# Second layer's values one step sooner, seven conv steps earlier, ScalarE's weight parts behind the transposes' copy, spatial products' halves by turns

## The chip, the cores and the metric

The kernel runs on one core of a Trainium2 chip. The metric is the device time of one execution in microseconds (us), the median of several runs. TensorE (PE) multiplies, ScalarE (ACT) and VectorE (DVE) do the element-wise work, GpSimd (POOL) helps a little, and SyncE (SP) issues most of the DMAs. Each engine runs its own instructions strictly in program order and waits on semaphores for the others.

## The reference

Two blocks follow each other. The first is one hybrid layer (dilated attention and a gated recurrence). The second has two layers on 512 tokens and 256 context tokens. The change touches the token mixers of the second block, which do this in each layer:

```
zx = split(hx @ w_in, 10)                    # ten parts of 256 columns
glu = a_val * sigmoid(a_gate)
y_a = silu(layer_norm(depthwise_conv(glu, conv_a_w) + b))        # 31 taps
p1 = softmax(q1 @ k1 * scale); p2 = softmax(q2 @ k2 * scale)
y_b = rms_norm(((p1 - lam * p2) @ v), subln_g) * (1 - lam_init)  # 4 heads
s   = einsum('gpq,bcqgd->bcpgd', w_s, layer_norm(gelu(v)))       # 4 groups of 64
y_c = gelu(u) * (s + b_s)
y_d = bg * depthwise_conv(cg * xin, conv_w)
x   = x + gate * (concat(y_a, y_b, y_c, y_d) @ w_out)
```

Layer 0 of the block also runs the mixers on the 256 context tokens; layer 1 only takes keys and values from them.

## The kernel before

**Weights.** Every large weight matrix comes in chunks of 1 MB (128 partitions x 2048). SP loads chunk n into a ring of three. `split(n)` exists twice: on ScalarE (L2107) it copies the chunk to a high part `whi` in reduced precision, and on VectorE (L2317) it subtracts that from the chunk and gets the low part `wlo`. So VectorE's `split(n)` waits for ScalarE's `split(n)` (semaphore `w_hi`), and PE waits for both before chunk n. Each product takes three matmuls (high x high, low x high, high x low), all recorded at L1957.

**Attention among the projections.** Chunks 5 to 9 of the input projection (j = 5 to 9) are cut into 16 steps each, 80 in all; a step is three matmuls of 512 columns (in layer 0 also three of 256 for the context). `fill(g)` puts attention work before step g. The attention of a layer is cut in units, one for 128 queries of one head: 16 in layer 1 (four a head), 20 in layer 0 (a fifth one a head for the context, with narrower tiles). A unit v starts at step `start(v)`, three steps after the one before it. On PE it has three pieces:

- `scores` at start - 3 (L624 to L627): four matmuls, q1 k1 and q2 k2. It waits for both exponentials of the unit before (`q_e`).
- `turn` at start + 2 (L643): six transposes of the combined probabilities. It waits for `combine` of its unit (`q_w`) and for the output of the unit before to be stored (`q_on`).
- `values` at start + 4 (L652, context units L658): twelve short matmuls. It waits for the copy of the transposes (`q_pt`).

Between them VectorE takes the maxima (L1351), ScalarE two exponentials with sums (L964, `exp(v, 0)` and `exp(v, 1)`), VectorE combines (L1365, L1366, L1371), ScalarE copies the transposes (L991, `out`) and stores the result scaled (L981, `scaled`). A round of ScalarE's loop `run` is `exp(v+1, 0)`, `scaled(v-1)`, `exp(v+1, 1)`, `out(v)`. A round of VectorE's is `combine(v)`, `maxima(v+1)`, then either a waiting weight split or three steps of the 31-tap convolution (L1247), whose 62 steps also fill earlier gaps. The units run in two batches: the first `cut` units (15 in layer 0, 12 in layer 1), and after the norms and spatial products the rest.

**Evictions.** `upto(g)` in ScalarE's and VectorE's loops empties the accumulators of the projection when its steps are due; after the second half of a chunk ScalarE calls `split(n + 2)` at once, while VectorE only notes it and does it after the next `maxima` (`weights_due`).

**Spatial products.** `s_mixed` (L703) multiplies a 64-column weight tile with 128 columns for each token block j and group g; groups 0 and 2 write partitions 0 to 63, groups 1 and 3 write 64 to 127. All j of one group come first, then the next group.

Of the kernel before, what the change touches and what calls it, by code (L numbers as in the profile page):

```python
# [157 lines left out]
class Plan:  # L158
# [21 lines left out]
        return self.start(v) + 2  # L180

    def values(self, v):
        return self.start(v) + 4


PLAN = [Plan(_l) for _l in range(L2)]
# [84 lines left out]
def build(nc, wst, mst, cbt, vec, xrs, xin, cin, gst, cst, msk, rop, row, sgw, sgb, out):  # L271
    with ExitStack() as ctx:
# [305 lines left out]
        def layer(pe, l, gemm, norm_sums, norm_spread, wait_high, wait_low, weights, step, half_gemm,  # L578
# [5 lines left out]
            nj = 6 if l == 0 else 4  # L584
# [110 lines left out]
            def s_mixed():  # L695
                pe.wait_ge(s_nat, l + 1)
                pe.wait_ge(m_t, 2 * l + 2)
                for c in (1, 0):
                    for g in (2 * c, 2 * c + 1):
                        half = 64 * (g % 2)  # L700
                        for j in range(nj):
                            o = (turned, score)[c][half:half + 64, j * P:(j + 1) * P]
                            last = pe.matmul(o, snat[:, j, 64 * g:64 * g + 64], wsT[:, g, :], start=True, stop=True)  # L703
                    last.then_inc(s_mix, 1)

            def fill(g):


                for v in range(p.units):
                    if g == p.scores(v):  # L710
                        scores(v)
                    if g == p.values(v):
                        values(v)
                    if g == p.turned(v):
                        turn(v)
                if g == p.mean:
                    means()
                if g == p.sums:
                    variances()
                if g == p.spread:  # L720
                    spread()
                if g == p.mix:
                    s_mixed()
# [147 lines left out]
        def layer_act(act, l, split, norm_square, norm_root, norm_high, mod_shift, half_square, half_root,  # L871
# [47 lines left out]
            def evict(j, c):  # L919


                n = base + j
                if j == 5:
                    act.wait_ge(qk_kept[0], 32 * (l + 1))
                    act.wait_ge(stacked[0], 16 * stacks_in(l, 0))
                    act.wait_ge(acc_ready[c], n + 1)
                    if two and c:
                        act.activation(svn[:, 4:6, :], ctx_acc, ACT.Copy).then_inc(ctx_out, 1)
                    act.activation(svn[:, 2 * c:2 * c + 2, :].rearrange("p b f -> p (b f)"), acc[:, c, 0:T], ACT.Copy
                                   ).then_inc(acc_free[c], 1)  # L930
                elif j < 8:
                    dst = (ug, cx)[j - 6]
                    o = 1 if j == 7 else 0
                    if j == 6:
                        act.wait_ge(qk_kept[1], 32 * (l + 1))
                    if j == 7:
                        act.wait_ge(cx_zero, l + 1)
                    act.wait_ge(acc_ready[c], n + 1)
                    if two and c:
                        oc = T + (3 if j == 7 else 0)  # L940
                        act.activation(dst[:, :, oc:oc + TC], ctx_acc, ACT.Copy).then_inc(ctx_out, 1)
                    act.activation(dst[:, c, o:o + T], acc[:, c, 0:T], ACT.Copy).then_inc(acc_free[c], 1)
                if c and j < 9:
                    split(n + 2)

            done = [0]

            def upto(g):


                while done[0] + 8 < g and done[0] < 80:
                    done[0] += 8
                    evict(5 + (done[0] - 8) // 16, (done[0] - 8) // 8 % 2)
# [49 lines left out]
            def run(v0, v1):  # L1003


                for part in range(2):
                    exp(v0, part)
                for v in range(v0, v1):
                    if v + 1 < v1:
                        exp(v + 1, 0)  # L1010
                    if v > v0:
                        scaled(v - 1)
                    if v + 1 < v1:
                        exp(v + 1, 1)
                    if p.turned(v) < 80:
                        out(v)

            run(0, p.cut)
            scaled(p.cut - 1)
# [4 lines left out]
            ins.then_inc(gelus, 1)  # L1024
            act.activation(ug[:, :, 0:wx], ug[:, :, 0:wx], ACT.Gelu_apprx_tanh).then_inc(gelus, 1)
            upto(p.mean)
            act.wait_ge(m_cen, l + 1)
            act.activation(sqm[:, :, 0:wx], yca[:, :, 0:wx], ACT.Square).then_inc(m_sq, 1)
            act.activation(unread[:, l:l + 1], epsc, ACT.Sqrt)
# [8 lines left out]
            act.wait_ge(sv_squared, l + 1)  # L1038
            act.activation(sv_sd[:, 0:nj], sv_sq[:, 0:nj], ACT.Sqrt, bias=epsc, scale=1.0 / GW).then_inc(sv_root, 1)
            upto(p.sums)  # L1040
            root_o(0)
            upto(p.spread)

            def affine(c, src, func, g, b):
                act.activation(src[:, c, 0:wx], src[:, c, 0:wx], func, bias=vcol(b, c, 1), scale=vcol(g, c, 1)
# [2 lines left out]
            for c in range(2):  # L1048
                act.wait_ge(m_t, 2 * l + c + 1)
                affine(c, yca, ACT.Silu, f"lag{l}", f"lab{l}")  # L1050
            upto(p.mix)
            run(p.cut, p.units)
            upto(89)

            def y_high(i):

# [135 lines left out]
        def layer_dve(dve, link, l, split, norm_inverse, norm_scale, modulate, modulation, coefficients,  # L1192
# [59 lines left out]
            for j in range(5):  # L1252
# [17 lines left out]
                if j > 2:  # L1270
                    rotate(j - 3)
                    if j == 4:
                        split(n + 1)
                    low(j - 3)
                    conv((7, 9)[j - 3] if two else 11)
                if j < 3:
                    split(n + 2)

# [1452 lines left out]
```

## Time and profile before

| | us |
|---|---|
| runs | 2112.39, 2116.89, 2120.92 |
| median | 2116.89 |
| profiled execution | 2115.37 |
| its span | 2113.5 |
| PE busy in the span | 2040.2 |

The span runs from the first to the last instruction; 1.87 us of the profiled execution lie around it. Busy times of matmuls contain their pipelined tails, so a busy PE may still have room. The attention of layer 0 lies at 712 to 871 us of the span, that of layer 1 at 1573 to 1694 us.

### The profile page before, as it was taken

What the parts mean: (1) busy time and instruction counts of PE and PEld (TensorE: products, weight loads), DVE (VectorE), ACT (ScalarE), POOL (GpSimd) and SP (SyncE); (2) the same over time, 40 slices, a digit from 0 to 9 for tenths busy, and PEclk for the clock granted to TensorE, in tenths of its full rate; (3) what the DMA queues carried; (4) which work ended last, traced back from release to release, by engine and by line L of the source; (5) the groups of instructions that cost most, each with busy time, mean ns of one, the idle gap of its engine ahead of it and who ended that gap; (6) DMA issues with size and microseconds to landing.
All of it is one profiled execution on the core that took longest, in us unless ns stands there. A gap on an engine that the chain in (4) does not pass through costs nothing.

```text
span 2113.5 us, 26503 instructions
## 1 busy us (share of the span) xinstructions
PE 2040.2 (97%) x11156; PEld 1739.0 (82%) x11156; DVE 1270.3 (60%) x1696; ACT 795.1 (38%) x1117; POOL 72.4 (3%) x81
## 2 busy tenths in 40 slices
PE   6999999999999999999999999999998999999998
PEld 5989888778788888887888888888787787888887
DVE  7466866867657885727546455464689645344343
ACT  4333334584343455534113122132536534132231
POOL 0000000000120000020000000001100010000001
PEclk9999999999999999999999999999999999999999
DMA  8643523525322531222333232232353122232221
GB/s 290 224 159 120 213 86 129 186 90 188 131 100 74 162 92 70 70 82 98 111 111 120 90 120 100 100 122 105 112 167 90 70 90 89 91 100 100 100 95 65
DMA packets 54054, 249.18 MB, mean 118 GB/s; under 512 B 6224, under 2 KB 12512, under 8 KB 35504
## 3 DMA queue, kind: packets, MB, share of 16 engines
q1 hardware_dynamic: 52048, 242.41, 33.4%
q10 hardware_dynamic: 1296, 2.63, 0.3%
q0 software_dynamic: 592, 2.46, 0.3%
q8 instruction: 88, 1.44, 0.3%
q14 instruction: 30, 0.25, 0.0%
HBM read 232.53 MB, written 12.06 MB: 116 GB/s over the span
## 4 chain that ended last, share of the span: by engine, by line
PE 85%; DVE 9%; ACT 3%; issue 2%; DMA 1%; POOL 0%; ACTq 0%; DVEq 0%; POOLq 0%
PE banks L1957 70%; DVE small L1351 2%; PE banks L1981 1%; PE banks L1982 1%; PE banks L1983 1%; PE banks L652 1%; PE banks L531 1%; ACT whi_f L2107 1%; PE banks L643 1%; DVE wlo_f L2317 1%; DVE ntx L2351 1%; PE banks L607 1%; PE banks L606 1%; PE banks L608 1%; PE banks L2013 1%
## 5 line engine op out<-in xcount | busy, mean ns | idle before, releaser
L1957 PE MATMUL banks<-hxh,whi_f 128*128 128x512 f32 (+1 forms) x1464 | 585.4, 400 | 24.3 <-ACT hxh L2136 7.5
L1957 PE MATMUL banks<-hxh,wlo_f 128*128 128x512 f32 (+1 forms) x1464 | 569.7, 389 | 0.0
L1957 PE MATMUL banks<-hxl,whi_f 128*128 128x512 f32 (+1 forms) x1464 | 555.2, 388 | 0.2 <-DVE hxl L2386 0.2
L2317 DVE TENSOR_TENSOR wlo_f<-raw_f,whi_f 128x2048 fp32r<-128x2048 f32 x133 | 304.9, 2293 | 181.4 <-ACT whi_f L2107 181.2
L2107 ACT ACTIVATE whi_f<-raw_f 128x2048 fp32r<-128x2048 f32 x133 | 253.7, 1907 | 308.3 <-PE banks L1957 290.1
L1957 PEld LDWEIGHTS banks<-hxh,whi_f 128*128 128x128 f32 x1464 | 276.1, 189 | 86.6 <-issue 27.5
L1957 PEld LDWEIGHTS banks<-hxh,wlo_f 128*128 128x128 f32 x1464 | 275.8, 188 | 57.9
L1957 PEld LDWEIGHTS banks<-hxl,whi_f 128*128 128x128 f32 x1464 | 274.9, 188 | 58.0 <-issue 1.9
L1957 PE MATMUL banks<-fxh,whi_f 128*128 128x512 f32 (+1 forms) x528 | 205.6, 389 | 2.1 <-DVE cT L1495 1.1
L1957 PE MATMUL banks<-fxh,wlo_f 128*128 128x512 f32 (+1 forms) x528 | 204.2, 387 | 0.0
L1957 PE MATMUL banks<-fxl,whi_f 128*128 128x512 f32 (+1 forms) x528 | 203.5, 385 | 0.0
L1495 DVE SCALAR_TENSOR_TENSOR xT<-banks,small,xT 128x512 f32<-128x512 f32 x76 | 56.5, 750 | 239.4 <-PE banks L1957 239.4
L1569 DVE TENSOR_TENSOR fsq<-relu 128x768 f32<-128x768 f32 (+1 forms) x64 | 52.7, 824 | 165.5 <-ACT relu L1149 165.5
L1149 ACT ACTIVATE relu<-banks 128x768 f32<-128x768 f32 (+1 forms) x64 | 45.1, 704 | 281.6 <-PE banks L1957 281.6
L1957 PE MATMUL banks<-hch,whi_f 128*128 128x256 f32 x464 | 132.7, 286 | 0.0
L1957 PE MATMUL banks<-hch,wlo_f 128*128 128x256 f32 x464 | 130.5, 281 | 0.0
L1957 PE MATMUL banks<-hcl,whi_f 128*128 128x256 f32 x464 | 130.0, 280 | 0.0
L1957 PEld LDWEIGHTS banks<-fxh,whi_f 128*128 128x128 f32 x528 | 99.2, 188 | 28.0 <-issue 4.8
L2337 DVE SCALAR_TENSOR_TENSOR mvr<-mvr,c2b 128x1024 f32<-128x1024 f32 x96 | 117.1, 1220 | 0.0
L1957 PEld LDWEIGHTS banks<-fxl,whi_f 128*128 128x128 f32 x528 | 99.2, 188 | 20.8
L1957 PEld LDWEIGHTS banks<-fxh,wlo_f 128*128 128x128 f32 x528 | 99.2, 188 | 20.4
L1247 DVE SCALAR_TENSOR_TENSOR aconv<-gpad,vecs,aconv 128x798 f32<-128x798 f32 (+1 forms) x120 | 99.6, 893 | 0.0
(340 smaller groups left out, 3129.3 us busy)
## 6 DMA issues: line engine op xcount, KB each, us to landing
raw_f<-in_wst SPq DMA_DIRECT2D x133, 1024.0 KB, 4.9
mvr<-in_mst SPq DMA_DIRECT2D x120, 512.0 KB, 5.8
stack<-qk_parts SPq DMA_DIRECT2D x36, 192.0 KB, 6.6
x_kept<-xT SPq DMA_DIRECT2D x2, 2048.0 KB, 8.6
raw_f<-in_wst SPq DMA_DIRECT2D x8, 384.0 KB, 5.9
xT<-x_kept SPq DMA_DIRECT2D x2, 1536.0 KB, 8.7
qk_parts<-qk_h SPq DMA_DIRECT2D x3, 768.0 KB, 3.8
qk_parts<-qk_l SPq DMA_DIRECT2D x3, 768.0 KB, 3.6
```

What stands on the lines that cost most here:

```text
L531: last = pe.matmul(at_ov, vb[h // 2][:, i, j, d], pt[:, u % 2, b * P:(b + 1) * P], start=(b == 0), stop=(b == 5))
L606: pe.matmul(place(b), hi[:, k, o:o + P], wh[:, k, :], start=(k == 0), stop=False)
L607: pe.matmul(place(b), lo[:, k, o:o + P], wh[:, k, :], start=False, stop=False)
L1149: act.activation(relu[:, c, 0:wx], acc[:, c, 0:wx], ACT.Relu).then_inc(acc_free[c], 1)
L1247: ins = dve.scalar_tensor_tensor(aconv[:, c, 0:wc], gpad[:, c, tap:tap + wc], w, aconv[:, c, 0:wc], ALU.mult, ALU.add)
L1351: dve.tensor_reduce(dnm[:, z:z + 2], score.rearrange("p (i k) -> p i k", i=2), AX_X, ALU.max, negate=True).then_inc(q_m, 1)
L1495: ins = dve.scalar_tensor_tensor(x_, acc[:, c, o:o + w], small[:, bass.ds(2 * t + g0, 1)], x_, ALU.mult, ALU.add)
L1569: dve.tensor_tensor(fsq[:, c, 0:wx], relu[:, c, 0:wx], relu[:, c, 0:wx], ALU.mult).then_inc(f_sq, 1)
L1957: last = pe.matmul(o, (wh, wl)[w][:, k, c, :], r[part][:, k, :], start=(k == order[0] and parts is not LOW and (w, part) == (0, 0)), stop= ...
L2107: act.activation(whi[n % 2 if n > N_FIRST else n][:], raw[w_place(n)][:], ACT.Copy).then_inc(w_hi, 1)
L2317: dve.tensor_tensor(wlo[r][:], raw[r][:], whi[n % 2 if n > N_FIRST else n][:].bitcast(F32), ALU.subtract).then_inc(w_lo, 1)
L2337: dve.scalar_tensor_tensor(w, w, 1.0, c2[:, 1], ALU.mult, ALU.mult, accum_out=mvc[:, col + 1:col + 2]).then_inc(mv_used, 1)
```

## The change

There are five edits.

1. In layer 1 `values(v)` moves from start + 4 to start + 3. At that step `scores(v+2)` also stands; `fill` now goes over all scores first, so that scores come ahead of the values.
2. In layer 1 ScalarE does `scaled(v-1)` ahead of `exp(v+1, 0)`; in layer 0 it stays between the exponentials.
3. ScalarE's `split(n + 2)` in chunks 5 to 8 is no longer done at the eviction: it is noted and done at `weights_due`, which stands at the end of a round of `run` behind `out(v)`, and at some places between the batches. VectorE's code for its own splits is as before.
4. In layer 1 the convolution does 14 and 15 steps instead of 11 and 11 during chunks 3 and 4, so seven fewer are left for the attention's rounds.
5. `s_mixed` loops over j outside and the two groups inside, so that the two halves of the partitions come by turns.

```diff
     def values(self, v):
-        return self.start(v) + 4
+        return self.start(v) + (4 if self.per == 5 else 3)
...
                 for c in (1, 0):
-                    for g in (2 * c, 2 * c + 1):
-                        half = 64 * (g % 2)
-                        for j in range(nj):
+                    for j in range(nj):
+                        for g in (2 * c, 2 * c + 1):
+                            half = 64 * (g % 2)
...
                 for v in range(p.units):
                     if g == p.scores(v):
                         scores(v)
+                for v in range(p.units):
                     if g == p.values(v):
                         values(v)
...
                 if c and j < 9:
-                    split(n + 2)
+                    weights_due()
+                    due[0] = n + 2
+
+            due = [None]
+
+            def weights_due():
+                if due[0] is not None:
+                    split(due[0])
+                due[0] = None
...
                 for v in range(v0, v1):
+                    if v > v0 and not two:
+                        scaled(v - 1)
                     if v + 1 < v1:
                         exp(v + 1, 0)
-                    if v > v0:
+                    if v > v0 and two:
                         scaled(v - 1)
                     if v + 1 < v1:
                         exp(v + 1, 1)
                     if p.turned(v) < 80:
                         out(v)
+                    weights_due()
...
-                    conv((7, 9)[j - 3] if two else 11)
+                    conv((7, 9)[j - 3] if two else (14, 15)[j - 3])
```

`weights_due()` is also called on ScalarE after `upto(p.mean)`, `upto(p.sums)`, `upto(p.spread)`, `upto(p.mix)` and `upto(89)`.

PE in layer 1, one round of the first batch. `whi_f,hxh` and the two beside it are the projection's step, `stack` the scores, `consts,prob` the transposes, `vnat,ptd` the values. Before:

```order
L643 MATMUL banks<-consts,prob 128x128 [waits diff_on,diff_pt,diff_w]
L643 MATMUL banks<-consts,prob 128x128 x5
L1957 MATMUL banks<-hxh,whi_f 128x512
L1957 MATMUL banks<-hxl,whi_f 128x512
L1957 MATMUL banks<-hxh,wlo_f 128x512
L624 MATMUL banks<-stack_127 128x512 [waits diff_e]
L625 MATMUL banks<-stack_127 128x256
L626 MATMUL banks<-stack_127 128x256
L627 MATMUL banks<-stack_127 128x512
L1957 MATMUL banks<-hxh,whi_f 128x512
L1957 MATMUL banks<-hxl,whi_f 128x512
L1957 MATMUL banks<-hxh,wlo_f 128x512
```

The values came behind that last step. Now the place from the scores on reads:

```order
L625 MATMUL banks<-stack_127 128x256
L626 MATMUL banks<-stack_127 128x256
L627 MATMUL banks<-stack_127 128x512
L652 MATMUL banks<-vnat,ptd 128x64 [waits diff_pt]
L652 MATMUL banks<-vnat,ptd 128x64 x5
L1976 MATMUL banks<-hxh,whi_f 128x512
L1976 MATMUL banks<-hxl,whi_f 128x512
L1976 MATMUL banks<-hxh,wlo_f 128x512
```

Two steps of the projection now stand between the values and the next transposes, where one stood before.

ScalarE in layer 1 at the end of chunk 6 (`ug` is its eviction), where the high part of chunk 8 is due; the two `prob` rows are the exponentials of unit 10, the `ptd` row behind them is the copy of unit 9's transposes, and `onat` is `scaled(8)`. Before:

```order
L942 ACTIVATE ug<-banks 128x512 [waits acc_ready1,qk_kept1]
L2107 ACTIVATE whi_f<-raw_f 128x2048 [waits acc_ready1,w_loaded1]
L964 ACTIVATE prob,small<-banks,small 128x768 [waits diff_t,diff_m]
L981 ACTIVATE onat<-banks,small 128x64 [waits diff_o]
L964 ACTIVATE prob,small<-banks,small 128x768
L991 ACTIVATE ptd<-banks 128x768 [waits diff_o,diff_t]
```

Now:

```order
L943 ACTIVATE ug<-banks 128x512 [waits acc_ready1,qk_kept1]
L992 ACTIVATE onat<-banks,small 128x64 [waits diff_o]
L975 ACTIVATE prob,small<-banks,small 128x768 [waits diff_t,diff_m]
L975 ACTIVATE prob,small<-banks,small 128x768
L1002 ACTIVATE ptd<-banks 128x768 [waits diff_o,diff_t]
L2126 ACTIVATE whi_f<-raw_f 128x2048 [waits acc_ready1,w_loaded1]
```

The high part went from ahead of unit 10's exponentials to behind them and behind the copy. Layer 0 has the same move at its chunk 6, with the same units.

VectorE at that place, the same before and now (line numbers of the changed kernel): the maxima of unit 10, the low part of chunk 8, the combining of unit 10.

```order
L1370 TENSOR_REDUCE small<-banks 128x2 [waits diff_s]
L2336 TENSOR_TENSOR wlo_f<-raw_f,whi_f 128x2048 [waits w_hi]
L1384 RECIPROCAL small<-small 128x2 [waits diff_on,diff_e]
L1385 SCALAR_TENSOR_TENSOR small<-small 128x1 [waits dve_step]
L1390 SCALAR_TENSOR_TENSOR prob<-prob,small 128x768 [waits dve_step]
```

Nothing moved here: the low part, which waits for the high part, stands ahead of unit 10's combining.

## Rows read from the trace of the kernel before

**Rows 1.** The page, part 1: engine, busy us, share of the span, instructions.

```profile
PE 2040.2 (97%) x11156; PEld 1739.0 (82%) x11156; DVE 1270.3 (60%) x1696; ACT 795.1 (38%) x1117; POOL 72.4 (3%) x81
```

**Rows 2.** PE's waits at 1560 to 1640: us in total, times, longest.

```profile
PE banks L643 <- ACT onat L981: 4.6, 9, 0.9
PE banks L624 <- ACT prob L964: 3.1, 2, 1.6
```

**Rows 3.** Timeline, layer 1, one round: start, us, engine, line, instruction [idle before <- releaser].

```profile
1594.39 0.17 DVE L1365 RECIPROCAL small<-small 128x2 f32<-128x2 f32 x1 [0.16 <-ACT prob L964]
...
1595.02 0.40 PE L624 MATMUL banks<-stack 128*128 128x512 f32 x1
...
1595.93 1.76 DVE L1351 TENSOR_REDUCE small<-banks 128x2 f32<-128x1536 f32 x1
...
1597.72 0.90 ACT L964 ACTIVATE prob<-banks,small 128x768 f32<-128x768 f32 x1 [2.40 <-DVE small L1351]
...
1598.61 0.30 ACT L981 ACTIVATE onat<-banks,small 128x64 f32<-128x64 f32 x1
...
1599.06 0.85 PE L643 MATMUL banks<-consts,prob 128*128 128x128 f32 x6 [0.42 <-ACT onat L981]
...
1599.83 0.17 DVE L1365 RECIPROCAL small<-small 128x2 f32<-128x2 f32 x1
```

**Rows 4.** Timeline, layer 1: two combinings with no `onat` row between them.

```profile
1578.60 0.15 DVE L1365 RECIPROCAL small<-small 128x2 f32<-128x2 f32 x1
...
1583.66 0.17 DVE L1365 RECIPROCAL small<-small 128x2 f32<-128x2 f32 x1
```

**Rows 5.** Timeline, layer 1, units 10 and 11 of the first batch.

```profile
1629.13 1.91 ACT L2107 ACTIVATE whi_f<-raw_f 128x2048 fp32r<-128x2048 f32 x1
...
1631.07 2.29 DVE L2317 TENSOR_TENSOR wlo_f<-raw_f,whi_f 128x2048 fp32r<-128x2048 f32 x1
...
1639.94 1.45 PE L652 MATMUL banks<-vnat,ptd 128*128 128x64 f32 x12
...
1641.98 0.82 PE L643 MATMUL banks<-consts,prob 128*128 128x128 f32 x6
```

**Rows 6.** Timeline, layer 0, unit 10 of the first batch.

```profile
773.28 1.93 ACT L2107 ACTIVATE whi_f<-raw_f 128x2048 fp32r<-128x2048 f32 x1
...
776.76 2.28 DVE L2317 TENSOR_TENSOR wlo_f<-raw_f,whi_f 128x2048 fp32r<-128x2048 f32 x1
...
778.96 0.60 ACT L991 ACTIVATE ptd<-banks 128x512 f32<-128x512 f32 x1
778.99 0.17 DVE L1365 RECIPROCAL small<-small 128x2 f32<-128x2 f32 x1
...
784.05 0.85 PE L643 MATMUL banks<-consts,prob 128*128 128x128 f32 x6 [0.40 <-ACT onat L981]
```

**Rows 7.** Timeline of VectorE alone, layer 1, chunks 3 to 5.

```profile
1555.72 0.69 DVE L1223 SCALAR_TENSOR_TENSOR tmp<-banks,rope 128x512 f32<-128x512 f32 x1 [2.74 <-issue]
...
1563.58 7.37 DVE L1247 SCALAR_TENSOR_TENSOR aconv<-gpad,vecs,aconv 128x512 f32<-128x512 f32 x11
1574.72 1.76 DVE L1351 TENSOR_REDUCE small<-banks 128x2 f32<-128x1536 f32 x1 [3.77 <-PE banks L627]
```

**Rows 8.** Timeline, layer 1: two runs of PE with 64-column weight tiles.

```profile
1647.85 0.66 PE L676 MATMUL banks<-wsT,consts 128*64 128x128 f32 x8
...
1660.21 2.57 PE L703 MATMUL banks<-wsT,snat 128*64 128x128 f32 x32
```

**Rows 9.** Windows: stretch, its us, busy us of PE, PEld, DVE, ACT, POOL, granted clock, DMA.

```profile
868.40:871.90 3.50, 1.83 (x13) 1.49 (x13) 2.72 (x6) 3.50 (x9) 0.00 (x0) 1.00 0.96 372
871.90:875.30 3.40, 3.40 (x11) 2.92 (x12) 3.40 (x7) 3.35 (x7) 0.00 (x0) 0.50 0.91 352
875.30:878.70 3.40, 3.40 (x21) 2.94 (x20) 3.30 (x8) 3.16 (x5) 0.00 (x0) 1.00 0.02 5
1576.00:1579.40 3.40, 1.79 (x13) 1.50 (x13) 3.33 (x5) 1.88 (x4) 0.00 (x0) 1.00 1.05 259
```

More of the change, by code:

```diff
@@ L1026, in layer_act @@
             upto(p.mean)
+            weights_due()
             act.wait_ge(m_cen, l + 1)
@@ L1040, in layer_act @@
             upto(p.sums)
+            weights_due()
             root_o(0)
             upto(p.spread)
+            weights_due()
             def affine(c, src, func, g, b):
@@ L1051, in layer_act @@
             upto(p.mix)
+            weights_due()
             run(p.cut, p.units)
             upto(89)
+            weights_due()
             def y_high(i):
```

## The prediction

> **What bounds the kernel now.** I read the page first: PE is busy for 2040.2 of 2113.5 us [rows 1]. What it does not idle away cannot be won by moving work of the other engines, so the waits of PE are all there is to gain. Next its waits in layer 1's first batch of attention: nine times 4.6 us before the transposes (`turn`) on the stored output of the unit before, and 3.1 us before the scores of units 1 and 2 on the exponentials [rows 2]. Then the timeline of one round, to see what sets its length. The reader should follow the circle there: VectorE combines from 1594.39, takes the next maxima from 1595.93, ScalarE starts `exp` at 1597.72, stores the output at 1598.61 (0.20 us between its start and the second `exp`), and the next combining starts at 1599.83, 5.44 us after the last [rows 3]. Where no output is stored between the exponentials, a round takes 1583.66 - 1578.60 = 5.06 us [rows 4]. PE has slack: the transposes wait 0.42 us [rows 3]. So a round in layer 1 is bound by the circle VectorE - ScalarE, with PE close behind.
>
> **Edits 1 and 2 in layer 1, the gain.** The output is stored while ScalarE waits 2.40 us for the maxima [rows 3], so the 0.20 us leave the circle. The values end earlier by a step, so that this output is ready in that gap. What is late next is the circle itself at 5.06 us: combining 1.4, maxima 1.8, two exponentials 1.85. PE's own work per round is 5.44 less the wait of 0.42, so 5.0 us at most; it just fits. The round shortens by 0.38 us. Eight rounds lie between unit 2 and unit 10; an eviction between the exponentials (about 0.5 us in two of them) leaves the circle too, and one round carries a weight split on VectorE and gains little. 7 x 0.38 + 2 x 0.5 = 3.7 us; at unit 10 PE and VectorE should be about 3.5 us ahead of before. The bounds: nothing, if PE's switch between kinds of work keeps it at 5.4, and the 4.6 us of waits at most. In the second batch I find 0.3 us for the few rounds and give back as much at its end, since the values now come so soon behind the transposes that they wait about 0.4 us for the copy (0.8 us). That is 0.
>
> **Edit 3, the move that costs.** ScalarE's high parts have four places per layer in question. At three of them the high part moves by a copy or a norm's worth of work and VectorE asks for it only later; I cost them at nothing, since the low parts there stand behind maxima or norms that end later anyway. The fourth is chunk 6's end, unit 10, in both layers. Before, the high part starts at 1629.13 and the low part on VectorE at 1631.07, right after the maxima, in the time in which ScalarE takes the exponentials [rows 5]. Now the high part stands behind both exponentials and the copy, while the low part still stands ahead of the combining of unit 10. VectorE therefore waits on that semaphore, and queued behind it are the combining, the next maxima and all that hangs on them; PE's next transposes wait for the combining.
>
> Layer 0: the copy starts at 778.96 and takes 0.5 us on ScalarE; the high part (1.93) then ends at 781.4, the low part (2.28) at 783.7 where the combining now starts at 778.99 [rows 6]. Then 1.4 combining, 1.8 maxima, 0.9 for the first `exp`, and, since layer 0 keeps the output behind that `exp`, 0.6 until PE may turn: 788.4 against 784.05 [rows 6]. PE had 0.40 us of waiting there, which is in the 784.05. So **+4.4 us**, all on the path, as nothing later in that layer waits long enough to give it back.
>
> Layer 1, with the 3.5 us of head start: unit 10's exponentials 1627.8 to 1629.7, copy to 1630.5, high part to 1632.4, low part to 1634.7, combining to 1636.2 (PE has waited 3 us at the transposes). The maxima of unit 11 and its exponentials end at 1639.7, the copy of unit 10 at 1640.5, and only then come the values of unit 10, which before started at 1639.94 [rows 5] (PE waits another 3 us). From the values to the next transposes lie 1.25 + two steps of 0.7 + 0.1, so they start at 1643.2 instead of 1641.98 [rows 5]. The values of unit 11 wait 0.4 us for their copy. Sum **+1.6 us**: the head start of 3.5 is spent and more. Without the head start it would be +5.1.
>
> **Edit 4.** Three steps at chunk 3 and four at chunk 4. A step is 7.37 / 11 = 0.67 us [rows 7]. VectorE idles 2.74 us ahead of the rotation at 1555.72 and 3.77 us ahead of the first maxima at 1574.72 [rows 7]: 2.0 and 2.7 us fit. Nothing is paid; without that cover it would be 4.7 us. In the rounds the steps ran beside the exponentials, so removing them from units 8 on brings nothing either. **0**.
>
> **Edit 5.** 32 records of `s_mixed` take 2.57 us, of which the last one's own length is 0.27: 2.30 / 31 = 0.074 us each. The 8 records at L676 already have their halves by turns: (0.66 - 0.27) / 7 = 0.056 us each [rows 8]. Layer 0 has 48 records and layer 1 has 32: 80 x 0.018 = 1.5 us. I take **-1.5**, with 0 and -3 as ends (no effect; half of all), as L676 is the nearest row: same tile, same columns. The Trainium skill (TensorEngine Tiling (Array Packing), Key Properties) says that different tiles can load weights and multiply in parallel, up to twice as fast by its table; by that rule the edit would bring some 3 us, and L676 with 0.056 rather than 0.037 speaks for less.
>
> **The clock.** In this trace the granted clock fell to 0.50 at 871.9 to 875.3, after a stretch of 3.5 us in which PE was busy for 1.83 us only; 11 matmuls ran there and 21 in the equal stretch behind it, so it cost half of 3.4, 1.7 us [rows 9]. At 1576.0 PE was busy for 1.79 of 3.4 us and the clock stayed [rows 9], so the fall is not certain. The three new waits (4.7, 3 and 3 us) are emptier than either stretch. The middle one has another wait behind it that hides a slow stretch. I take one fall on the path, **+1.7**, with 0 and 5 as ends. The Trainium skill (TensorE: Matmul & The Clock Gate, Why this matters for your kernels) warns of gaps in PE's work for this reason; the trace agrees at 871.9.
>
> **Sum.** 4.4 + 1.6 + 0 + 0 - 1.5 + 1.7 = +6.2 us. Against the profiled execution, 2115.4 + 6.2 = 2121.6 us (span 2119.7 and 1.87 around it). That execution lies 1.5 below the median of the runs, 2116.9, and the runs spread from 2112.4 to 2120.9, so 1.5 more or less is in the measure of before itself.
>
> **The rivals.** *Forecast:* the low part waits behind the late high part in both layers and eats more than the shorter rounds give. For it speaks the order of the rows on both engines, which nothing at run time changes. 2121.6, own range 2117 to 2126.
>
> *The rounds win.* If PE were not held by VectorE at unit 10 (its transposes of unit 10 being covered by something that I count as serial), the stalls would vanish and the rest stay: -3.5 (edit 1 and 2) - 1.5 = -5.0, 2110.4. Against it: PE's slack per round is 0.4 us and the delay 4.7. A half of it, the stall in layer 0 only, gives 2115.4 + 4.4 - 3.5 - 1.5 = 2114.8.
>
> *The clock falls for longer.* At the three new waits, and once more in layer 1, PE runs at half clock for a stretch of 3.4 us behind each: 4 x 1.7 = 6.8 instead of 1.7, and the head start in layer 1 is only half (+1.8). 4.4 + 3.4 - 1.5 + 6.8 = +13.1, 2128.5. It decides from the fourth stretch on, since two falls give 2123 and three 2125. For it: three waits of a kind that the trace of before does not have. Against it: the waits of 1.6 us before units 1 and 2 left the clock alone.
>
> *The edit does less than it says.* Rounds stay at 5.4 and the halves by turns bring nothing: 4.4 + 5.1 + 1.7 = +11.2, 2126.6.
>
> **How the numbers follow.** Forecast 0.62, the edit does less 0.12, the clock for longer 0.11, the rounds win or half of it 0.15. The likeliest is 2121.6 us. For the range I leave out the full win (below 2112) and the longest clock falls: 2112.5 to 2128. About 0.5% of the time, 10.6 us, is what a measurement can tell from no change: faster needs less than 2106.3, which no case reaches (0.02 for what I overlook); slower needs over 2127.5, the clock's case and the upper tail of the one before it (0.15); the same, 0.83.
>
> **What would show it.** In layer 1 the distance from one combining to the next should read about 5.1 us instead of 5.44 up to unit 9, with the output's row in the gap ahead of the exponentials. At unit 10 of each layer VectorE should idle 4 us or so ahead of the low part, released by ScalarE's high part, and PE 3 to 5 us ahead of the transposes. The seven convolution steps should leave idle time of 0.7 and 1.1 us where they now stand. `s_mixed` should take 1.8 to 2.0 us in layer 1. A clock of 0.50 should stand behind the wait in layer 0. The prediction is wrong if VectorE's low part finds its high part ready, or if the transposes of unit 10 start on time.

## The result, and the profile after

The kernel after takes **2129.6 us** (median of 5 runs, 2126.5 to 2131.4) against 2120.2 us for the kernel before (5 runs): ratio 1.0048, interval 1.0032 to 1.0064. Run once more on another chip it was 2131.0 against 2119.0 (1.0059, 1.0044 to 1.0073). It is slower by 0.5%, and lies above the forecast of 2121.6 and above the whole range (2112.5 to 2128.0). The profiled execution took 2126.5, its span 2124.7 against 2113.5 before.

The whole kernel on one line, page part 1, to set beside [rows 1]:

```profile
PE 2048.7 (96%) x11156; PEld 1748.2 (82%) x11156; DVE 1270.1 (60%) x1696; ACT 795.6 (37%) x1117; POOL 72.5 (3%) x81
```

PE has the same 11156 instructions and is *busy* for 8.5 us longer. Waits would show as idle time; busy time that grows for the same instructions means that some of them ran slower. That is the first sign of where the prediction fell short.

PE's waits of the kernel after at 1560 to 1700 (us in total, times, longest), to set beside [rows 2]:

```profile
PE banks L624 <- ACT prob L975: 6.2, 4, 1.7
PE banks L643 <- DVE prob L1390: 2.5, 1, 2.5
PE banks L652 <- ACT ptd L1002: 2.2, 4, 1.5
```

Between 1560 and 1700 the kernel before waits 6.2 us for `prob` ahead of the scores, as here, and 5.8 us in eleven waits for `onat` ahead of the transposes. Those waits for `onat` are gone, as forecast. A round at units 8 and 9 (timeline: start, us, engine, line, instruction [idle before <- releaser]), to set beside [rows 3]:

```profile
1615.60 0.17 DVE L1384 RECIPROCAL small<-small 128x2 f32<-128x2 f32 x1
...
1617.92 0.32 ACT L992 ACTIVATE onat<-banks,small 128x64 f32<-128x64 f32 x1 [1.65 <-PE banks L652]
...
1618.77 0.90 ACT L975 ACTIVATE prob<-banks,small 128x768 f32<-128x768 f32 x1 [0.54 <-DVE small L1370]
...
1620.68 0.17 DVE L1384 RECIPROCAL small<-small 128x2 f32<-128x2 f32 x1
```

From combining to combining are 5.08 us instead of 5.44, and the output is stored in the gap ahead of the exponentials. Now unit 10, layer 0 first, then layer 1 (timeline), beside [rows 6] and [rows 5]:

```profile
783.39 1.91 ACT L2126 ACTIVATE whi_f<-raw_f 128x2048 fp32r<-128x2048 f32 x1
785.33 2.29 DVE L2336 TENSOR_TENSOR wlo_f<-raw_f,whi_f 128x2048 fp32r<-128x2048 f32 x1 [4.55 <-ACT whi_f L2126]
787.54 0.16 DVE L1384 RECIPROCAL small<-small 128x2 f32<-128x2 f32 x1
...
792.25 1.09 PE L643 MATMUL banks<-consts,prob 128*128 128x128 f32 x4 [4.66 <-ACT onat L992]
...
1636.49 1.91 ACT L2126 ACTIVATE whi_f<-raw_f 128x2048 fp32r<-128x2048 f32 x1
1638.44 2.29 DVE L2336 TENSOR_TENSOR wlo_f<-raw_f,whi_f 128x2048 fp32r<-128x2048 f32 x1 [4.44 <-ACT whi_f L2126]
1640.64 0.16 DVE L1384 RECIPROCAL small<-small 128x2 f32<-128x2 f32 x1
1642.17 1.54 PE L643 MATMUL banks<-consts,prob 128*128 128x128 f32 x6 [2.50 <-DVE prob L1390]
...
1646.44 1.55 PE L652 MATMUL banks<-vnat,ptd 128*128 128x64 f32 x12 [1.46 <-ACT ptd L1002]
```

VectorE idles 4.5 us ahead of the low part in both layers, released by the late high part, and PE waits behind it. And the windows of the kernel after (stretch, its us, busy us of PE, PEld, DVE, ACT, POOL, granted clock, DMA), beside [rows 9]:

```profile
741.00:744.40 3.40, 1.73 (x10) 1.62 (x11) 2.96 (x9) 2.01 (x7) 0.00 (x0) 0.94 0.94 355
744.40:747.80 3.40, 3.40 (x15) 2.97 (x14) 0.00 (x0) 2.61 (x2) 0.00 (x0) 0.56 1.03 225
747.80:751.20 3.40, 3.40 (x25) 3.13 (x24) 3.21 (x2) 1.42 (x4) 0.00 (x0) 1.00 0.72 157
788.40:791.80 3.40, 0.00 (x0) 0.00 (x0) 3.40 (x4) 1.09 (x4) 0.00 (x0) 1.00 0.00 0
791.80:795.20 3.40, 2.95 (x11) 2.76 (x12) 3.06 (x5) 2.00 (x5) 0.00 (x0) 0.50 0.00 0
...
1638.30:1641.70 3.40, 1.36 (x6) 0.75 (x5) 3.19 (x4) 0.31 (x2) 0.00 (x0) 1.00 0.31 66
1641.70:1645.10 3.40, 2.82 (x9) 2.00 (x9) 2.08 (x2) 1.29 (x3) 0.00 (x0) 0.50 0.00 0
1645.10:1648.50 3.40, 2.06 (x15) 1.97 (x16) 1.40 (x3) 1.60 (x4) 0.00 (x0) 1.00 0.00 0
1648.50:1651.90 3.40, 3.40 (x13) 2.85 (x12) 0.00 (x0) 1.09 (x2) 0.00 (x0) 0.51 0.02 5
```

A fall of the clock to 0.50 (1.2 of 2.4 GHz) stands behind the wait in layer 0, and two stand behind the waits in layer 1. In all there are **ten** such falls of 3.4 us in this execution (at 611, 744, 792, 833, 881, 1591, 1642, 1649, 1686 and 1771), against the one at 871.9 in the profiled execution before. The fall at 744 follows a wait of 2.1 us for ScalarE's `svn` that the kernel before has too; so not every fall is the change's. The falls at 611 and 833 follow no wait of PE over 0.3 us at all (see the last section). To split luck from cause I used the mean granted clock that each run lists, and experiments.

Laid side by side by VectorE's instructions, the two profiled executions differ like this (after minus before): +0.7 at 600; +4.0 at 760 (the falls at 611 and 744, 1.6 us each); +8.2 right behind the low part of unit 10 and +9.6 behind the fall at 792; +9.2 at 890; +5.4 at 1440 (see the last section); +9.1 at 1660, behind layer 1's first batch; +8.5 behind `s_mixed`; +9.6 at 1700; +11.2 at 1780, behind the fall at 1771, and at the end.

### The profile page after: what moved, and what is told of

The parts are those of the page before. It is cut to its first block, busy times and chain, and to the rows that moved or that the text cites. A ratio compares the mean times of both kernels' runs of the same rounds, so it can differ in the third digit from the quotient of the medians.

```text
span 2124.7 us, 26503 instructions
## 1 busy us (share of the span) xinstructions
PE 2048.7 (96%) x11156; PEld 1748.2 (82%) x11156; DVE 1270.1 (60%) x1696; ACT 795.6 (37%) x1117; POOL 72.5 (3%) x81
## 4 chain that ended last, share of the span: by engine, by line
PE 84%; DVE 9%; ACT 3%; issue 2%; DMA 1%; POOL 0%; ACTq 0%; DVEq 0%; POOLq 0%
PE banks L1976 69%; DVE small L1370 2%; PE banks L2000 1%; PE banks L2001 1%; PE banks L2002 1%; PE banks L652 1%; PE banks L531 1%; ACT whi_f L2126 1%; DVE prob L1390 1%; DVE wlo_f L2336 1%; DMA mvr<-in_mst 1%; DVE aconv L1266 1%; PE banks L606 1%; PE banks L607 1%; PE banks L608 1%
```

## The experiments

Each kernel ran beside the kernel before on one chip; kernels with the same value under "before" shared it. The ratio is not that of the two medians but lies near that of the means; where a kernel's runs are spread wide (e5, e7), the two readings differ by up to 2 us. "Clock" is the mean granted clock over a kernel's timed runs; for the kernel before it was 0.9950 to 0.9954 in the four sets. Over 277 runs of all kernels, a run's distance from its kernel's mean time goes with its distance from its kernel's mean clock at 1.8 us (plus or minus 0.1) for each 0.001 (correlation -0.74), and one fall of 3.4 us is 0.0008 of the clock: some 1.5 us.

| kernel | median us | before | ratio (interval) | clock |
|---|---|---|---|---|
| after, first set | 2129.6 | 2120.2 | 1.0048 (1.0032 to 1.0064) | 0.9906 |
| e0 before again | 2118.7 | 2118.2 | 1.0005 (0.9994 to 1.0017) | 0.9951 |
| e1 edit 3 undone | 2119.2 | 2118.2 | 1.0008 (0.9996 to 1.0019) | 0.9925 |
| e2 edit 3 alone | 2132.4 | 2118.2 | 1.0072 (1.0055 to 1.0089) | 0.9912 |
| e3 edit 3 but at chunk 8 | 2116.2 | 2118.2 | 0.9992 (0.9982 to 1.0003) | 0.9929 |
| e4 edit 5 alone | 2117.9 | 2120.0 | 0.9979 (0.9966 to 0.9992) | 0.9958 |
| e5 edits 1, 2 alone | 2122.7 | 2120.0 | 1.0001 (0.9985 to 1.0016) | 0.9935 |
| e7 low part a round later | 2118.9 | 2120.0 | 0.9984 (0.9968 to 0.9999) | 0.9939 |
| e9 after, waits filled | 2126.3 | 2120.0 | 1.0027 (1.0011 to 1.0042) | 0.9934 |
| e10 after again | 2131.0 | 2119.0 | 1.0059 (1.0044 to 1.0073) | 0.9896 |
| e8 stall in layer 1 only | 2121.9 | 2119.0 | 1.0010 (0.9998 to 1.0023) | 0.9922 |
| e11 as e9 | 2126.5 | 2119.0 | 1.0044 (1.0029 to 1.0060) | 0.9924 |
| e6 edit 4 alone | 2118.7 | 2119.0 | 1.0004 (0.9991 to 1.0016) | 0.9948 |
| e12 e7, first values as before | 2113.3 | 2119.0 | **0.9974 (0.9964 to 0.9984)** | 0.9954 |
| e13 as e7 | 2118.1 | 2119.0 | 0.9993 (0.9983 to 1.0002) | 0.9931 |
| e14 e7 without edits 1, 2 | 2117.2 | 2119.0 | 0.9992 (0.9981 to 1.0002) | 0.9945 |

**e0, the kernel before again.** No edit.

> The kernel before, unchanged, profiled once more. Its first profiled execution had a mean granted clock of 0.998 and one fall to 0.50 in the middle of the kernel (871.9 us); the kernel after had 0.991 and ten. Theory 'the change brings the falls': this one shows 0.997 or more and at most two falls, whatever its time. Rival 'falls come by themselves': the clock lies between 0.991 and 0.996, with three or more falls at places that no new wait explains, and the time is 2118 to 2121 instead of 2115.4. Ratio 1.000 either way.

The profiled execution has the clock at 0.995 and falls at 823 (twice as long), 878 and 1499, and the 12 runs average 0.9951. So the rival holds half: the kernel before has some four falls in a run by itself (estimated from its mean clock and that of this execution), and its first profiled execution, with one, was a lucky one. But the kernel after has more, ten on average by its 0.9906 and 0.9896; 0.005 more clock is lost, at 1.8 us for each 0.001 some 9 us.

**e1, e2 and e3: where edit 3 costs.** e2 is the kernel before with edit 3 alone. e1 takes edit 3 back out of the kernel after; e3 does so only where chunk 6 ends:

```
                 if c and j < 9:
-                    weights_due()
-                    due[0] = n + 2
+                    split(n + 2)               # e1

                     weights_due()
                     due[0] = n + 2
+                    if j == 6:                 # e3
+                        weights_due()
```

> The kernel after with edit 3 taken back (ScalarE makes the high part right behind the eviction, as before); edits 1, 2, 4 and 5 stay. Theory 'the late high part': no wait of 4 us or more ahead of the low part or the transposes at unit 10 of either layer, and the gain of the shorter rounds (3.5) and of the halves by turns (1.5) remains: 5 us under the kernel before (ratio 0.9976, about 2114). Rival 'the clock, whatever the edits': ten falls stay, and the time is within 2 us of before or above it. Rival 'another edit costs': above before by 3 us or more.

> The kernel before with edit 3 alone. Theory 'the late high part': +4.4 us in layer 0 and +5.1 us in layer 1 (no head start), and 1.7 to 5 us of slow clock behind the waits: +11 to +14 us, ratio 1.0055, longer than the kernel after although it has one edit only. Rival 'the edits add up to the loss by other ways': +4.4 or less, ratio 1.002.

> The kernel after, but at the end of chunk 6 (unit 10, in both layers) the high part is made at once as before; at the other chunks it stays behind the transposes' copy. Theory 'only that place costs': the same time as with edit 3 taken back in full, within 2 us (5 us under before). Rival 'the three other places cost too, which the prediction put at nothing': 2 us or more above it.

e2 costs 14.3 us, just above what its theory said: edit 3 alone is dearer than all five edits. e3 is 2.0 us *under* before by the medians, though its interval (0.9982 to 1.0003) takes in no change, and 5 us under were expected; its clock is 0.0024 below before's, which at 1.8 us for each 0.001 is 4.3 us. So the whole loss sits at that one place, unit 10 of both layers, and the gain that was left over went mostly into the clock. But e1, which has no late high part at all, comes out at +1.0 where -5 was expected, 3 us over e3 on the same chip. The prediction had costed the three other places at nothing; they are worth something to edits 1 and 2. The timeline of e1 at the end of chunk 5 of layer 1 shows how (copy, values and output are those of unit 3, the exponentials behind them unit 5's):

```profile
1601.90 1.92 ACT L2125 ACTIVATE whi_f<-raw_f 128x2048 fp32r<-128x2048 f32 x1
...
1603.70 0.81 ACT L1001 ACTIVATE ptd<-banks 128x768 f32<-128x768 f32 x1
...
1604.57 2.82 PE L652 MATMUL banks<-vnat,ptd 128*128 128x64 f32 x12 [2.01 <-ACT ptd L1001]
...
1607.43 0.31 ACT L991 ACTIVATE onat<-banks,small 128x64 f32<-128x64 f32 x1 [2.91 <-PE banks L652]
1607.64 0.89 ACT L974 ACTIVATE prob<-banks,small 128x768 f32<-128x768 f32 x1
```

The high part stands ahead of the copy, the copy ahead of the values, the values ahead of the stored output, and (by edit 1) that output ahead of the next exponentials. Each link waits for the last; PE waits 2.0 us, and here the clock fell for twice 3.4 us on top.

**e4, e5 and e6: the edits one at a time.** e4 is edit 5 (loop over `j` outside the loop over `g` in `s_mixed`), e5 is edits 1 and 2, e6 is edit 4, each put alone into the kernel before.

> The kernel before with edit 5 alone (halves by turns in s_mixed, both layers). Theory: 80 records at 0.018 us less, -1.5 us, mean granted clock as in the kernel before (0.995): ratio 0.9993. Rival 'packed matmuls leave a longer or emptier stretch and cost the clock': clock 0.994 or less and no gain.

> The kernel before with edits 1 and 2 alone (layer 1's values a step sooner, output stored ahead of the exponentials); the high part at once as before. Theory 'the two edits need edit 3': at units 6 and 10 the copy waits behind the high part, the values behind the copy, and now the exponentials behind the stored output, so that a round of 6.6 us or more stands where 5.1 was expected; the gain of 3.5 shrinks to 1 or less and the clock falls there: ratio 0.999 to 1.001. Rival 'the forecast': 3.5 us under before, ratio 0.9983.

> The kernel before with edit 4 alone (seven convolution steps of layer 1 at chunks 3 and 4 instead of in the rounds). The prediction's term: 0, within 1.5 us of before, clock as before (0.995), and layer 1's rounds still 5.44 us long. Rival: the steps delay the rotation or the first maxima, +2 us or more.

e4 gains 0.2%, 2.1 us by the medians, of which some 1.3 (an estimate) are its higher clock, 0.0007, and its timeline, first layer 0 and then layer 1, gives the sizes without the clock:

```profile
834.51 2.84 PE L703 MATMUL banks<-wsT,snat 128*64 128x128 f32 x48
...
1666.14 1.97 PE L703 MATMUL banks<-wsT,snat 128*64 128x128 f32 x32
```

Layer 1 took 2.57 us [rows 8], so 0.60 less; layer 0 took 4.29 in the kernel before, so 1.45 less. Edit 5 is worth 2.0 us. e5 behaves as the theory of the expectation says: no gain (1.0001), a mean clock of 0.9935, and at the end of chunk 5 the same wait of 2.0 us for the copy of unit 3 (not of unit 6, as the expectation has it). e6 is what was forecast: its VectorE instructions keep the distance to the kernel before, 1.74 us ahead of the moved steps (at 1540) and 1.75 behind them, and its rounds are unchanged.

**e7 and e8: the stall by itself.** In e7 ScalarE's high part stays late, but VectorE makes the low part of chunk 8 one round later, behind the maxima of unit 11. e8 is the kernel after with the high part at once in layer 0 only.

```
-                    splits = due[0] is not None
-                    weights_due()
+                    splits = due[0] is not None and (due[0] != base + 8 or held[0])
+                    held[0] = due[0] == base + 8
+                    if splits:                  # e7
+                        weights_due()
```

> The kernel after, with the low part of chunk 8 on VectorE one round later (behind the maxima of unit 11) in both layers; ScalarE's high part stays late. Theory 'VectorE's wait for the late high part is the stall': the waits of 4.4 to 4.7 us at unit 10 are gone in both layers, 11 to 13 us under the kernel after, so 2116 to 2118, mean clock 0.993, like the kernel with the high part of that chunk at once. Rival 'ScalarE's own load at unit 10 is the stall': the waits stay at 2 us or more and the time is 2122 or more.

> The kernel after, with the high part of chunk 8 made at once in layer 0, as before; layer 1 keeps it late. The prediction's terms: layer 0 costs 4.4, its fall 1.7, so 6.1 us under the kernel after; what is left over the kernel without the late part of chunk 8 (e3) is layer 1's stall, 5.1 (1.6 and the spent head start of 3.5), plus a fall or two: 5 to 8. Rival 'layer 1 was sized too low': 9 us or more over e3. Rival 'layer 0': less than 4 us under after.

e7 takes all of the loss away: it is 0.2% under before in this set, and e13, the same kernel in another set, 0.1% (0.9 us by the medians, where 2 to 4 were expected). Layer 1, timeline of VectorE from the maxima of unit 10 to its combining, first in e7, then in e8:

```profile
1628.20 1.75 DVE L1370 TENSOR_REDUCE small<-banks 128x2 f32<-128x1536 f32 x1
...
1631.89 0.17 DVE L1384 RECIPROCAL small<-small 128x2 f32<-128x2 f32 x1 [1.94 <-ACT prob L975]
```

```profile
1624.72 1.75 DVE L1372 TENSOR_REDUCE small<-banks 128x2 f32<-128x1536 f32 x1
...
1630.91 2.29 DVE L2338 TENSOR_TENSOR wlo_f<-raw_f,whi_f 128x2048 fp32r<-128x2048 f32 x1 [4.44 <-ACT whi_f L2128]
1633.12 0.16 DVE L1386 RECIPROCAL small<-small 128x2 f32<-128x2 f32 x1
```

3.69 us against 8.40: the stall in layer 1 is 4.7 us, and the same distance between the two kernels still stands at 1700. Layer 0's stall is the distance between e8 and e10: 4.3 us right behind it, 5.7 behind the fall at 792 and 7.1 behind the one at 833, of which e8 has neither (the one at 833 has its like in e0, which has no stall). By the medians e8 is 9.1 us under e10, with 0.0026 more clock: 4.3 of stall and some 4.7 of clock. Expected were 6.1 under the kernel after, and 5 to 8 over e3; by the ratios to before it is 3.8 us over e3. So the theory missed both of its sizes, and neither rival of that expectation names what came; it was the prediction's term for the stall that held and its term for the fall that did not.

**e10, e9 and e11: is it the clock?** e9 and e11 are the kernel after, stalls and all, but PE does work whose result is overwritten while it waits:

```
     def turn(v):
+        pe.wait_ge(q_pt, u0 + v)
+        for b in range((32, 18)[l] if v == 10 else 0):
+            pe.transpose(turned[:, b % 4 * P:(b % 4 + 1) * P], ident, ident)
         pe.wait_ge(q_w, u0 + v + 1)
-        pe.wait_ge(q_pt, u0 + v)
         pe.wait_ge(q_on, u0 + v)
```

> The kernel after, unchanged, once more. Theory 'the falls hang on its two stalls': mean clock 0.990 to 0.992, 9 to 11 us over before (ratio 1.0045 to 1.0055), and falls behind unit 10 of both layers again, whatever places the others take. Rival 'the first comparison caught an unlucky set': 0.993 or more and 5 us or less over before.

> The kernel after, with TensorE doing 32 (layer 0) and 18 (layer 1) transposes of the identity, whose result is overwritten, in the wait ahead of the transposes of unit 10: some 4.2 and 2.4 us of work in waits of 4.7 and 2.5. Theory 'half of the loss is the clock that falls behind these waits': the combinings come at the same distance as in the kernel after, but the clock stays up behind them; mean clock 0.992 to 0.993 instead of 0.9906, and 3 to 4 us less than the kernel after (2125 to 2126). Rival 'the falls do not hang on these waits': clock and time as in the kernel after, 2128 to 2130.

> The kernel after with the waits ahead of the transposes of unit 10 filled, once more, now beside the kernel after on one chip. Theory 'the clock behind the waits': 4 us under the kernel after, mean clock 0.002 to 0.003 above it. Rival: within 2 us of it.

Windows of e9 at unit 10 of layer 0, and behind the values of unit 10 of layer 1:

```profile
786.30:789.70 3.40, 3.40 (x34) 3.40 (x32) 3.33 (x6) 0.14 (x1) 0.00 (x0) 1.00 0.00 0
789.70:793.10 3.40, 2.24 (x17) 1.85 (x16) 3.33 (x6) 2.96 (x7) 0.00 (x0) 1.00 0.00 0
793.10:796.50 3.40, 3.40 (x25) 3.16 (x24) 3.40 (x4) 0.96 (x3) 0.00 (x0) 1.00 0.00 0
```

```profile
1646.20:1649.60 3.40, 0.70 (x6) 0.41 (x4) 1.39 (x4) 2.58 (x5) 0.00 (x0) 0.99 0.00 0
1649.60:1653.00 3.40, 3.40 (x15) 3.11 (x14) 0.34 (x1) 0.31 (x1) 0.00 (x0) 0.50 0.00 0
```

In layer 0 the clock stays at 1.00 where the kernel after had 0.50, in e9 and in e11; in layer 1 the wait that was not filled, 2.7 us ahead of the values, still brings a fall of twice 3.4 us in both. On one chip the filled kernel is under the kernel after by 4.5 us by the medians (2126.5 against 2131.0) and by 2.5 us by the means (2127.6 against 2130.1), with five runs each, so the size of the gain is not settled, and the intervals of the two ratios overlap. The clock is 0.0028 higher in this pair and by the same amount in e9 against the first set; at 1.8 us for each 0.001 that is 5 us. No way but the clock is in sight for a gain, since the filling only adds work: the stall stays, and VectorE still idles 4.55 us ahead of the low part of layer 0 (e9). Of the three or four falls that 0.0028 stands for, the profiles place one, that behind the stall of layer 0.

**e12, e13 and e14: the rest of the falls.** e7 has no new wait of over 0.7 us and still lost clock (0.9939 and, in e13, 0.9931). In e12 only the values of units 0 and 12 of layer 1 go back to their old step:

```
-        return self.start(v) + (4 if self.per == 5 else 3)
+        return self.start(v) + (4 if self.per == 5 or v in (0, self.cut) else 3)
```

> The kernel e7 (after, low part of chunk 8 one round later), with the values of the first unit of each batch of layer 1 (units 0 and 12) at their old step, so that after the wait ahead of the scores of the next unit but one the long products of the chunk come first again. Theory 'edit 1 brings falls because the short products of the values now stand right behind a wait of 1.5 us': mean clock 0.9945 to 0.9955 instead of e7's 0.9939, no fall at the scores of unit 2, and 1 to 2 us under e7 on the same chip. Rival: clock and time as e7 within 0.0004 and 0.8 us.

> The kernel e7 once more, as the measure for the other two on one chip: 2 to 4 us under before, clock 0.9935 to 0.9945.

> The kernel e7 without edits 1 and 2: high parts late, the low part of chunk 8 a round later, edits 4 and 5 in. Theory 'edits 1 and 2 give 2.8 us of rounds and cost a fall or two': clock 0.995, as before, and within 1.5 us of e7. Rival 'their clock is luck': clock as e7 and 3 us over e7.

PE of e13 behind its wait ahead of the scores of unit 2 in layer 1 (timeline), and its windows there:

```profile
1588.75 0.50 PE L624 MATMUL banks<-stack 128*128 128x512 f32 x1 [1.50 <-ACT prob L975]
...
1589.55 2.07 PE L652 MATMUL banks<-vnat,ptd 128*128 128x64 f32 x12
```

```profile
1586.80:1590.20 3.40, 1.90 (x15) 1.60 (x14) 3.33 (x7) 3.06 (x6) 0.00 (x0) 1.00 0.00 0
1590.20:1593.60 3.40, 3.40 (x18) 3.40 (x17) 3.40 (x5) 1.94 (x5) 0.00 (x0) 0.50 0.00 0
```

The same place in e12, where six matmuls of 256 columns come between:

```profile
1579.17 0.50 PE L624 MATMUL banks<-stack 128*128 128x512 f32 x1 [1.49 <-ACT prob L975]
...
1579.98 0.28 PE L606 MATMUL banks<-whi_f,hxh 128*128 128x256 f32 x1
...
1580.70 1.45 PE L652 MATMUL banks<-vnat,ptd 128*128 128x64 f32 x12
```

```profile
1577.20:1580.60 3.40, 1.91 (x15) 1.62 (x14) 3.33 (x8) 3.06 (x6) 0.00 (x0) 1.00 0.01 3
1580.60:1584.00 3.40, 3.40 (x32) 3.40 (x31) 3.40 (x5) 1.81 (x4) 0.00 (x0) 1.00 0.00 0
```

The wait is the same (1.5 us) and the busy time of PE around it is the same (1.9); what differs is that the values, twelve matmuls of 64 columns, came straight behind the scores. Of the ten profiled executions with edits 1 and 2 whose values stand there, eight have a fall at this place (1583 to 1595); of the seven without these edits or with e12's order, none has. One thing remains that this account does not cover. At 1760 to 1776, behind a wait of 2.1 us for the low part that every kernel has, the same ten all have a fall and the same seven none; e12 shows the same rows there as e13, without the fall. So the profile of e12 lacks two falls, and the order of the matmuls explains the first only. Whether the second hangs on the order or on when that wait comes, no run tells. The gain is larger than asked for: e12's clock is that of the kernel before, and it is 4.8 us under e13 by the medians (4.0 by the means, for 0.0023 more clock, which is all of it). It is also under the kernel before by 5.7 us, and under e14, which has no edits 1 and 2, by 3.9. **e12 is the version that beats both kernels.** e14's clock (0.9945) is near before's, as its theory says, and its time is within 1 us of e13: with the values straight behind the wait, edits 1 and 2 gave by the rounds what they took by the clock.

## Why the prediction was wrong

**What bounds the kernel, and edits 1 and 2.** Right, for the kernel with edit 3 in it. The rounds went from 5.44 to 5.08 us. Without a fall among them (e12 against e6, layer 1's first batch) they are worth 3.2 us where the forecast had 3.5. But what was credited to edits 1 and 2 needs edit 3: e5 gains nothing, since a high part ahead of the copy now holds up the exponentials as well.

**Edit 3.** The mechanism, the place and the size were right. Layer 0: 4.2 us against the forecast's 4.4. Layer 1: 4.7 against 5.1 without the head start, and 4.7 - 3.2 = 1.5 against the sum's 1.6; PE's waits there were 2.5 and 1.5 us where the forecast had 3 and 3. After minus before grew there by 3.7 us instead of 1.6, with two falls of the clock in the stall and one ahead of it. That the three other places cost nothing was right for the kernel before and an omission for this one: there the edit helps.

**Edit 4.** Right: 0.01 us, and VectorE's idle times of 2.74 and 3.77 us became 0.75 and 1.11, as forecast. **Edit 5.** 2.0 us instead of 1.5. The forecast took layer 1's 0.074 us a record for both layers; layer 0's 48 records took 4.29 us, so (4.29 - 0.27) / 47 = 0.086 each, and the end value of 0.055 is that of L676 in both.

**The clock, the step that failed.** The sum had "one fall on the path, **+1.7**", with 5 as the upper end. The terms without the clock, as measured, are 4.3 + 4.7 - 3.2 - 2.0 = +3.8 us; the two comparisons gave +9.4 and +12.0. So what is left for the clock is 5.6 to 8.2 us, and the lost 0.0045 to 0.0058 of mean clock, at 1.8 us each 0.001, give say 8 to 10. Three things were missing from the term. It counted a fall only where a wait is new, and took one for three waits: by e8 against e10 layer 0's stall alone went with 4.7 us of clock, and filling the waits gave back 2.5 to 4.5 (e11). It read from one profiled execution with one fall that waits of 1.6 us leave the clock alone [rows 9]; the kernel before has four falls on average, and in e0 those at 878 and 1499 stand behind waits of 1.4 and 2.2 us, while the long one at 823 has only a wait of 0.2 us ahead of it. And it did not ask what PE does behind a wait: edit 1 put the 64-column matmuls there, and with e12's order two or three falls go (0.0023 of clock). The Trainium skill (TensorE: Matmul & The Clock Gate, Why this matters for your kernels) warns of gaps of PE's work that are longer than any of the new waits but layer 0's; here falls followed waits of 1.5 and 2.1 us too, and the measurement decides. For the same reason the prediction's "the trace agrees at 871.9" said too much: the longest wait ahead of that fall was 1.41 us.

**The base.** The second part of the miss is the same error once more. The sum was added to the profiled execution, 2115.4 us, which had a clock of 0.998; over all sets the kernel before stands at 2118.2 to 2120.2 with 0.995. In the first comparison 4.8 of the 8.0 us by which the forecast missed are this base, and 3.2 the sum (+6.2 against +9.4). The prediction allowed 1.5 us for it.

**The rivals.** "The clock falls for longer" gave 2128.5 with a chance of 0.11 and came nearest, by its mechanism too. It was held down by "the waits of 1.6 us before units 1 and 2 left the clock alone", one execution's luck. The full or half win of the rounds is excluded by the stalls themselves, 4.3 us in layer 0 and 4.7 in layer 1. "The edit does less than it says" is excluded by the rounds of 5.08 us and by edit 5's 2.0.

## What to carry to other kernels

When ScalarE's part of a pair is moved later, move VectorE's part with it: in e7 one condition took away a stall of 4 to 5 us in each layer. Count a wait of TensorE with the slow stretch that can follow it, take how often the clock falls from several runs and not from one profile, and, where the order is free, try wide matmuls first behind a wait. An edit that makes one engine wait for another in a ring (here the output stored ahead of the exponentials) makes every instruction ahead of one link part of the ring, so it is to be measured with the order that it needs, not alone.

## What the runs showed of the hardware

The kernel before ran 116 times in the four sets, at mean granted clocks of 0.993 to 0.998, and its time went with them: 2123.4 us on average at 0.993 (six runs), 2112.6 at 0.998 (four).

The same places bring a fall in some executions and not in others. Of the seventeen profiles:

| place | what PE does ahead of it | profiles with a fall |
|---|---|---|
| 611 | sixteen matmuls of one column, wait of 0.3 us | 11 |
| 744 | wait of 2.1 us for `svn` | 5 |
| 823 to 834 | 24 matmuls of one column, wait of 0.2 us | 10 |
| 870 to 884 | waits of 0.5 and 1.4 us, 64-column matmuls | 16 |
| 1760 to 1776 | wait of 2.1 us for the low part | 10 |

I can't say from these traces what picks them. But a wait is not needed. PE of the kernel after (timeline, then windows) ahead of its fall at 833:

```profile
828.61 2.84 PE L684 MATMUL banks<-consts,sqm 128*128 128x1 f32 x24 [0.21 <-ACT sqm L1043]
...
829.40:832.80 3.40, 3.40 (x27) 3.22 (x27) 3.24 (x4) 3.39 (x14) 0.00 (x0) 0.99 0.00 0
832.80:836.20 3.40, 3.40 (x16) 3.21 (x15) 2.45 (x4) 2.33 (x7) 0.00 (x0) 0.51 0.00 0
```

By the records PE is busy throughout, with a run of one-column matmuls, and the clock falls all the same. So a PE that is busy in the records does not rule out a fall. This fits what e12 shows of the narrow matmuls, though no run changed these.

Transposes of the identity, 32 of them in 3.65 us, kept the clock at 1.00 through the stall of layer 0 (e9). The three profiles with that stall unfilled (the kernel after, e10, e2) have a fall there, the two with it filled (e9, e11) none.

The windows of one and the same stretch of feed-forward chunks, first in the kernel before, then in the kernel after:

```profile
1340.10:1391.80 51.70, 51.70 (x295) 44.82 (x294) 25.31 (x35) 11.72 (x14) 0.00 (x0) 1.00 0.31 112
```

```profile
1347.00:1397.80 50.80, 50.80 (x295) 44.41 (x295) 25.36 (x35) 11.73 (x14) 0.00 (x0) 1.00 0.32 114
```

The clock is 1.00 and PE busy throughout in both, and yet the stretch took 51.7 us in one and 50.8 in the other, with the same instructions. Such stretches gave back 4.5 us between 1000 and 1440 in the first pair of traces, and took 1.6 in the pair e0 and e10. No row shows a wait in them; the cause stays open, and it is one reason why two profiled executions don't settle a difference of a few us.
